# Expert gates of a two-block model: the one-hot rows times gate as two-tensor operations

## The reference

```
q = (h @ w_q).reshape(b, s, PEER_HEADS, 2, PEER_HALF)          # 8 heads, two halves
sc = einsum('bshpc,hpkc->bshpk', q, sub_keys)                  # 128 keys for each half
top_v, top_i = top_k(sc, 16)                                   # of each half
cand_v = top_v[..., 0, :, None] + top_v[..., 1, None, :]
best_v, best_pos = top_k(cand_v, 16)
idx = take_along_axis(top_i0 * 128 + top_i1, best_pos)         # expert = (i1, i2)
gate = softmax(best_v)
act = gelu(u_tab[idx] . h);   out = sum(gate * act * v_tab[idx])
```

## Time and profile before

| what | value |
|---|---|
| median of 3 runs | 1919.74 us |
| lowest, highest | 1917.58, 1919.88 us |
| profiled execution, its device time | 1918.82 us |
| profiled execution, its span from first to last instruction | 1917.0 us |
| PE busy in the span | 1834.7 us, 96% |
| DVE busy in the span | 1345.1 us, 70% |
| ACT, POOL busy in the span | 922.1 us, 315.6 us |

### The profile page before, as it was taken

The page is one execution under the profiler, slowest core; times in us unless marked ns, Lnnn a source line. Parts: engine busy times, 40 slices in busy tenths (PEclk is TensorE's granted clock), DMA queues, the critical chain, the costliest instruction groups (busy, mean ns, idle before and its releaser), DMA issues.

```text
span 1917.0 us, 30741 instructions
## 1 busy us (share of the span) xinstructions
PE 1834.7 (96%) x12639; PEld 1680.2 (88%) x12639; DVE 1345.1 (70%) x2055; ACT 922.1 (48%) x1238; POOL 315.6 (16%) x118
## 2 busy tenths in 40 slices
PE   7999999999999888899999999998999999989998
PEld 7999899999988888888888888888898889879887
DVE  5657876999788988955555556887667545657754
ACT  6457636444433333354444445676555443545533
POOL 0000003760555555510000000021000001100000
PEclk9999999999999999999999999998999999999999
DMA  6444345445433333355555554331055446635543
GB/s 231 176 155 159 132 176 202 173 176 176 140 127 131 132 132 133 127 186 204 196 197 192 187 191 159 133 131 67 13 178 183 181 192 215 175 116 202 190 164 151
DMA packets 44758, 310.66 MB, mean 162 GB/s; under 512 B 5182, under 2 KB 5694, under 8 KB 8160
## 3 DMA queue, kind: packets, MB, share of 16 engines
q1 hardware_dynamic: 42592, 303.58, 43.8%
q0 software_dynamic: 1472, 4.86, 1.4%
q10 hardware_dynamic: 576, 0.55, 0.1%
HBM read 306.84 MB, written 2.13 MB: 161 GB/s over the span
## 4 chain that ended last, share of the span: by engine, by line
PE 61%; DVE 17%; issue 4%; ACT 2%; POOL 0%; DVEq 0%; ACTq 0%
PE bank L1706 18%; PE bank L347 13%; PE bank L3035 9%; PE bank L358 6%; DVE s_hT L1958 5%; PE bank L362 3%; PE bank L1677 2%; PE bank L3294 1%; DVE s_arena L1846 1%; DVE s_ring_lo L310 1%; PE bank L446 1%; PE bank L2660 1%; DVE s_arena L1843 1%; DVE s_arena L1889 1%; DVE s_arena L2122 1%
## 5 line engine op out<-in xcount | busy, mean ns | idle before, releaser
L304 ACT ACTIVATE s_w_hi<-s_ring 128x2048 fp32r<-128x2048 f32 x244 | 465.7, 1909 | 133.3 <-PE bank L347 48.2
L310 DVE TENSOR_TENSOR s_ring_lo<-s_ring,s_w_hi 128x2048 fp32r<-128x2048 f32 x184 | 421.0, 2289 | 145.2 <-ACT s_w_hi L304 140.7
L347 PE MATMUL bank<-s_h_r,s_w_hi 128*128 128x256 f32 x3072 | 406.3, 285 | 0.3 <-DVE s_arena L3523 0.3
L347 PEld LDWEIGHTS bank<-s_h_r,s_w_hi 128*128 128x128 f32 x3072 | 382.9, 192 | 4.8 <-issue 3.6
L1834 POOL TENSOR_TENSOR s_ring_lo<-s_ring,s_w_hi 128x2048 fp32r<-128x2048 f32 x61 | 282.8, 4637 | 545.3 <-ACT s_w_hi L304 541.9
L1706 PE MATMUL bank<-s_w_hi,s_h_r 128*128 128x512 f32 x1008 | 238.7, 389 | 0.0
L347 PE MATMUL bank<-s_h_r,s_ring_lo 128*128 128x256 f32 x1536 | 217.7, 284 | 19.9 <-POOL s_ring_lo L1834 18.5
L1958 DVE TENSOR_SCALAR s_hT<-s_consts,s_slots 128x128 f32<-128x128 f32 x256 | 205.5, 864 | 38.7 <-PE bank L1677 38.7
L1706 PEld LDWEIGHTS bank<-s_w_hi,s_h_r 128*128 128x128 f32 x1008 | 189.2, 188 | 39.2
L347 PEld LDWEIGHTS bank<-s_h_r,s_ring_lo 128*128 128x128 f32 x1536 | 197.6, 192 | 24.6 <-POOL s_ring_lo L1834 22.8
L1806 ACT ACTIVATE s_h_r<-s_arena 128x512 fp32r (+1 forms) x64 | 40.4, 632 | 184.1 <-PE bank L1706 184.1
(11 more groups left out here) (464 smaller groups left out, 2500.6 us busy)
## 6 DMA issues: line engine op xcount, KB each, us to landing
s_ring<-weights SPq DMA_DIRECT2D x282, 1024.0 KB, 4.8
s_arena<-bias_by_distance POOLq DMA_DIRECT2D x12, 384.0 KB, 8.4
s_arena<-mem SPq DMA_DIRECT2D x1, 1024.0 KB, 5.8
s_x<-x SPq DMA_DIRECT2D x1, 1024.0 KB, 13.5
x_away<-s_x SPq DMA_DIRECT2D x1, 1024.0 KB, 7.8
s_arena<-sub_keys SPq DMA_DIRECT2D x1, 1024.0 KB, 10.7
s_arena<-x_away SPq DMA_DIRECT2D x1, 1024.0 KB, 8.4
out<-s_x SPq DMA_DIRECT2D x2, 512.0 KB, 2.6
```

Source lines behind the costliest of these rows:

```text
L304: act.activation(k.w_hi[:, u % 2, :], k.ring[:, u % RING, :], ACT.Copy).then_inc(k.hi_ready, 1)
L310: dve.tensor_tensor(k.ring_lo[:, u % RING, :], k.ring[:, u % RING, :], plain(k.w_hi[:, u % 2, :]), ALU.subtract).then_inc(k.lo_ready, 1)
L347: last = pe.matmul(out[:, nb * S:(nb + 1) * S], w[:, c, nb * P:(nb + 1) * P], h[:, c, :], start=(n == 0 and c == 0), stop=(n == 2 and c == 7))
```

## The change

The four instructions of `heat` that build the one-hot rows of i1 times the gate are written in another form. Before, each was a comparison of the iota row with i1 and a product with the gate, both given as per-partition scalars. After, i1 is still a per-partition scalar, and the gate is given as a second tensor, one column read with a step of zero 128 times. The result is the same.

```diff
@@ -1955,7 +1955,8 @@
                 dve.wait_ge(spread_mm, g - 1)
             for n in range(GROUP_T):
                 i1, gate = (slotsT[:, c, g * GROUP_T + n:g * GROUP_T + n + 1] for c in (0, 2))
-                dve.tensor_scalar(hot[:, g % 2, 0, n, :], k.iota, i1, gate, ALU.is_equal, ALU.mult)
+                dve.scalar_tensor_tensor(out=hot[:, g % 2, 0, n, :], in0=k.iota, scalar=i1,
+                                         in1=gate.to_broadcast([P, KEYS]), op0=ALU.is_equal, op1=ALU.mult)
             i2 = slotsT[:, 1, g * GROUP_T:(g + 1) * GROUP_T].rearrange("p (t n) -> p t n", n=1)\
                 .to_broadcast([P, GROUP_T, KEYS])
             dve.tensor_tensor(hot[:, g % 2, 1, :, :], over(k.iota, GROUP_T), i2, ALU.is_equal)\
```

## The result

The changed kernel takes 1924.34 us (median of 20 runs, 1920.0 to 1925.78), the kernel before 1920.09 us (median of 20, 1917.58 to 1923.19). The ratio is 1.002, with a 95% interval from 1.0013 to 1.0027: 2.5 to 5.2 us slower, around the bound of 0.2% that the prediction set for a difference. The forecast of +3.3 us lies in that interval, and 1924.34 us in its range.

The account below looks back on a forecast made before the run. In this stage the bound was taken to be a ring of POOL, DVE and ACT, not PE. Adding 0.166 us a turn over 20 turns gives 3.3 us: 1919.74 + 3.3 = 1923.0 us, range 1918.0 to 1926.5.

Parts of the forecast that it names:

- the bound of 0.2%: Smallest difference a measurement of this kernel tells from none, 3.8 us; the forecast of +3.3 us (0.17%) lay just inside.
- The new form is held too: In heat, the new instructions, with both tensors in SBUF, still wait for POOL's running instruction to end, like the old ones.
- The half rate behind POOL: The new form streams 128 elements at half the rate, so a held instruction ends 0.067 us later behind each POOL end.
- The free ones: Heat's instructions that POOL doesn't hold: each costs 0.003 to 0.009 us more from start to start, 0.005 taken.
- The sum: Per turn 0.074 before POOL's second instruction, 0.067 behind it, 0.025 for five free ones: 0.166 us, 3.3 over 20 turns.
- the ring: Chain of POOL, DVE and ACT that closes without PE, 16.28 us a turn; anything added to it counts 20 times.
- its signs: Profile checks: held instructions end 0.15 us behind POOL, POOL's second takes about 4.68, free ones about 0.345, turn grows 0.17.
- The full half rate: Rival: dropping the second scalar gives nothing back, 0.067 us eight times a turn, 10.7 us in all, 1930.4 us; chance 0.06.
- nothing: Rival: another edge, PE's unit or a weight load, sets POOL's start and absorbs the 0.166 us: 1919.7 us; chance 0.07.
- not held: Rival: the new form doesn't need what POOL occupies, so PE's waits go: 1887 us, or 1905 in part; chance 0.09.
- POOL gets in first: Rival: POOL's second instruction is served before heat's second, leaving three behind it: 0.27 us a turn, 5.5 us, 1925.2; chance 0.10.

Follow-up runs that it names:

- the third alone: Kernel before, with only the third of each heat's four gate instructions in the new form: 1923.32 against 1920.46 us, stage 1.40 us longer.
- the old form with one scalar: Kernel before, with the second scalar (the product with the gate) left out of the four instructions: 1913.55 against 1920.46 us, ratio 0.9955.
- the kernel with the second and fourth: Kernel before, with only the second and fourth of each heat's four instructions in the new form: 1920.29 against 1920.34 us, ratio 1.0003.
- the mixed ones: Kernel before with only some of the four in the new form; the two meant: first and third, 1924.8 against 1920.34 us; first only, 1923.05 against 1920.46.
- first-alone kernel: Kernel before, with only the first of each heat's four instructions in the new form: 1923.05 against 1920.46 us, ratio 1.0014.

## Why the prediction was right

*The new form is held too.* Shown: in the changed kernel it is held behind both low parts of each turn, and with one of its tensors in PSUM it isn't, in 256 of 256 instructions. The prediction named the reason as both tensors lying in SBUF, by L2122 and L2843 under the same POOL instruction.

The Trainium skill, SBUF — State Buffer, section Who interferes with whom, says that a VectorE instruction with two SBUF inputs contends with a GpSimd instruction that reads SBUF. The runs agree, with 1.44 us instead of 0.68 for the i2 rows under POOL, and 0.34 for the gate rows with one tensor in PSUM.

*The half rate behind POOL.* Predicted 0.067 us for each end of POOL. Shown by the third alone: 0.070 a turn, with the small price of one free one in it. In the traces the held instructions end 0.066 us later behind POOL than the old form (0.151 against 0.085). That this is the rate and not a fixed cost is borne out by the lengths: the old form with one scalar ends as far behind POOL as with two (0.083 and 0.085), though it is 58 ns shorter when free, and the i2 rows, with four times the elements of a gate row, end 0.55 us behind.

*The free ones.* Predicted 0.003 to 0.009 each, 0.005 taken. In the changed kernel four take 1.14 instead of 1.11 us, with a median of 347 against 340 ns for one, and the kernel with the second and fourth costs 0.55 us in all against 0.4.

*The sum.* 0.166 us a turn was predicted and 0.173 measured, 3.3 and 3.45 us in 20 turns. The parts agree too, by the medians over the turns: POOL's second low part is 0.070 longer (0.074 predicted), L1961's place behind POOL's end 0.075 later (0.072 for the held one and the free one after it), and the rest of the ring 0.03 longer (0.020 for four free ones). The medians of the runs differ by 4.25 us, and the 0.8 beyond the stage lie inside their interval of 2.5 to 5.2.

Two figures beside the sum don't follow from the prediction's own terms. Among its signs it wanted about 4.68 us for POOL's second low part, where 4.67 and the 0.074 of the sum give 4.74; 4.73 was measured. And half the spread of 2.3 us around its two ends gives a range of 1918.6 to 1926.4, not 1918.0 to 1926.5. The result lies in either.

*The ring.* That DVE's time counts although PE is busy 90% of the stage was argued from the chain and the timeline. It is shown from two sides: 58 ns less in each instruction shortens the stage by 8.2 us, and without the holding it shrinks to within 2.6 us of PE's busy time.

*The rivals.* "The full half rate" falls with the median of 347 ns, "nothing" with the longer stage, "not held" with the held ones. "POOL gets in first" didn't occur in the changed kernel, but it is real: it occurred in two of the mixed ones. Its price had been worked out as 0.27 us a turn for the new form; for the old form in second place it measured 0.20.

What the prediction had right with less ground than it thought was that order. It argued that the second instruction stays 0.06 us ahead of POOL, and that at another place one that began 0.04 behind POOL's start still went first. But that one was L1961, another form. In the changed kernel the second instruction was 0.07 ahead and went first; in the mixed ones an old form 0.07 ahead did not. So the lead alone doesn't decide, and that the changed kernel kept its order was in part luck: had POOL gone first, the prediction's own price for it was 5.5 us instead of 3.3.

## What to carry to other kernels

When a VectorE instruction is held behind GpSimd, going over from the form at double rate to one with two SBUF tensors is no way out. The two-tensor form with one tensor in PSUM is, and here it was worth 36.6 us against the kernel before, with one operand of 256 small instructions moved. Whether the old form would get free with an operand in PSUM was not run. Look for a group whose mean is far above its median, and for holding that no semaphore shows: the chain view went through PE in most turns, and the ring was seen whole only in the timeline of POOL beside DVE. The price of such an instruction is set by where it stands: at the end of what holds it, each 0.07 us counts in every turn, and it can cost three times as much (0.20 us) when it makes the next one miss its place.

## What the runs showed of the hardware that I hadn't expected

An instruction of DVE that starts just ahead of POOL's isn't safe. In the first-alone kernel the TENSOR_SCALAR at 561.44, 0.07 us ahead of POOL at 561.51, is held 4.75 us, and POOL takes 4.60, its time where nothing holds it. In the changed kernel the SCALAR_TENSOR_TENSOR at 561.21, also 0.07 ahead of POOL at 561.29, runs through in 0.34, and POOL takes 4.72. With the TENSOR_SCALAR 0.13 ahead (560.83 against 560.96) it goes first. In both cases of 0.07 the instruction before it was a new form that had just been let go. In the kernel with one scalar, in the turn that lost 1.54 us, a TENSOR_SCALAR 0.09 ahead behind a free one goes first, and so does the L1961 right behind it, which starts at 513.02, 0.11 after POOL. Whether the form at double rate asks later, or has to wait until the one before it has written, stays open; no run here tells the two apart.
